# Four leading modulation panels: DVE chain or TensorE column groups, with v and q multiplied in halves around them

## What is computed

```python
c_act = jax.nn.silu(c)
for l in range(DEPTH):
    mod = (c_act @ ada_w[l] + ada_b[l]).reshape(bsz, 6, 1, D_MODEL)
    sh1, sc1, g1, sh2, sc2, g2 = (mod[:, i] for i in range(6))
    h = rms_norm(x, norm1_g[l]) * (1.0 + sc1) + sh1
    # l == 0: even_mixer
    proj = h @ w_in
    u, v, q, k, vd = split_cols(proj, (SGU_WIDTH, SGU_WIDTH, DIFF_QK, DIFF_QK, DIFF_V))
    ...
    x = x + g1 * y
    h = rms_norm(x, norm2_g[l]) * (1.0 + sc2) + sh2
    x = x + g2 * grouped_moe(h, router_w, router_b, moe_w_gu[l], moe_w_down[l])
return rms_norm(x, final_g)
```

## Time and profile before

| | us |
|---|---|
| median of 3 runs | 1056.99 |
| lowest and highest of the 3 | 1055.16, 1057.19 |
| the profiled execution, whole | 1058.29 |
| its span, first to last instruction | 1056.2 |
| mean granted TensorE clock | 0.931 |
| PE busy, of the span | 951.6 |
| DVE busy | 416.0 |
| ACT busy | 171.0 |

### The profile page before, as it was taken

One profiled execution on the slowest core, in us unless ns is written; L12 is line 12 of the kernel. 1 busy time (PEld: TensorE's weight loads), 2 busy tenths in 40 slices (PEclk: granted clock), 3 DMA queues, 4 the chain that ended last, 5 costly groups with the idle time before them and its releaser, 6 DMA issues.

```text
span 1056.2 us, 13230 instructions
## 1 busy us (share of the span) xinstructions
PE 951.6 (90%) x5496; PEld 609.1 (58%) x5496; DVE 416.0 (39%) x984; ACT 171.0 (16%) x416; POOL 13.0 (1%) x51
## 2 busy tenths in 40 slices
PE   2799789899999899896999989898789999999994
PEld 2476544565555465453868777765466556555551
DVE  4856575442141311312796645534351111111112
ACT  2121120221111011101101312332201111111101
POOL 1000000000000000000000000000000000000000
PEclk8699899799999899898999988988879999999998
DMA  9996644667999999999377312280209899999931
GB/s 353 387 372 246 238 161 157 239 235 294 406 408 409 404 409 407 407 397 365 138 262 286 108 62 102 81 318 1 79 24 404 328 409 409 409 408 409 408 158 42
DMA packets 96081, 294.16 MB, mean 278 GB/s; under 512 B 2448, under 2 KB 3088, under 8 KB 96016
## 3 DMA queue, kind: packets, MB, share of 16 engines
q1 hardware_dynamic: 95184, 289.89, 71.4%
q10 hardware_dynamic: 688, 2.82, 0.7%
q0 software_dynamic: 144, 0.52, 0.1%
HBM read 292.18 MB, written 1.05 MB: 278 GB/s over the span
## 4 chain that ended last, share of the span: by engine, by line
PE 49%; issue 26%; DVE 11%; DMA 6%; SPq 6%; ACT 3%; POOL 0%; DVEq 0%; POOLq 0%
PE bank L630 13%; PE bank L626 9%; PE bank L815 8%; SPq L406 5%; DVE gb L1210 4%; DMA ring<-w_gu_dram 4%; PE bank L830 3%; PE bank L806 2%; PE bank L844 2%; PE bank L659 2%; PE bank L681 2%; PE bank L566 2%; PE bank L574 1%; DMA ring<-ada_w_dram 1%; PE bank L788 1%
## 5 line engine op out<-in xcount | busy, mean ns | idle before, releaser
L815 PE MATMUL bank<-ring,scr 128*64 128x256 f32 x2176 | 253.2, 387 | 9.5 <-DMA ring<-w_gu_dram 9.5
L815 PEld LDWEIGHTS bank<-ring,scr 128*64 128x64 f32 x2176 | 154.8, 139 | 102.1 <-issue 20.6
L630 PE MATMUL bank<-hT,ring 128*128 128x256 f32 x640 | 149.7, 396 | 0.0
L630 PEld LDWEIGHTS bank<-hT,ring 128*128 128x128 f32 x640 | 127.1, 200 | 19.1 <-issue 0.5
L830 PE MATMUL bank<-ring,scr 128*64 128x512 f32 x544 | 122.6, 592 | 0.0
L1210 DVE SCALAR_TENSOR_TENSOR gb<-ring,small,gb 128x512 f32<-128x512 f32 x140 | 105.5, 754 | 5.0
L1660 DVE TENSOR_TENSOR scr<-bank,scr 128x256 f32<-128x256 f32 x34 | 14.4, 424 | 202.7 <-ACT scr L1150 202.7
L806 PEld LDWEIGHTS bank<-scr,xh 128*128 128x128 f32 x576 | 68.5, 195 | 24.5 <-issue 22.0
L806 PE MATMUL bank<-scr,xh 128*128 128x128 f32 x576 | 74.8, 285 | 2.3 <-DVE scr L1632 2.3
L830 PEld LDWEIGHTS bank<-ring,scr 128*64 128x64 f32 x544 | 38.9, 137 | 64.4 <-issue 59.8
L1132 ACT ACTIVATE scr<-bank 128x256 f32<-128x256 f32 (+1 forms) x52 | 23.4, 450 | 300.1 <-PE bank L823 237.3
(11 more groups left out here) (217 smaller groups left out, 685.5 us busy)
## 6 DMA issues: line engine op xcount, KB each, us to landing
ring<-w_gu_dram SPq DMA_DIRECT2D x64, 2048.0 KB, 21.7
ring<-w_down_dram SPq DMA_DIRECT2D x32, 2048.0 KB, 21.1
ring<-ada_w_dram SPq DMA_DIRECT2D x24, 2048.0 KB, 18.1
ring<-od_w_in_dram SPq DMA_DIRECT2D x9, 2048.0 KB, 13.6
ring<-ev_w_in_dram SPq DMA_DIRECT2D x5, 2048.0 KB, 17.4
ring<-ev_w_out_dram SPq DMA_DIRECT2D x2, 2048.0 KB, 9.7
ring<-od_w_out_dram SPq DMA_DIRECT2D x2, 2048.0 KB, 11.0
xs<-x_dram ACTq DMA_DIRECT2D x1, 1024.0 KB, 6.1
```

What stands on the lines that cost most here:

```text
L630: ins = pe.matmul(banks[h][:, m * 256:(m + 1) * 256], w[:, c, (2 * h + m) * P:(2 * h + m + 1) * P], x_part[:, c, :], start=(c == 0 and m = ...
L815: ins = pe.matmul(b[64 * m:64 * m + 64, 256 * u:256 * u + 256], h[:, c, :], w[:, c, 512 * u + 256 * m:512 * u + 256 * m + 256], start=(fir ...
```

## The change

- **PE takes the four leading panels.** `ada_row(n)` multiplies a panel directly: eight matmuls, one for each chunk c, whose weights are the column `cact[:, c]` repeated 32 times and whose output is the 32 partitions `32 * (c % 4)` of bank 6. So the chunks go in turn to four column groups of the array, twice each. DVE copies the bank to SBUF (L1785), and `ada_row_sum` sums over the partitions as before, with a column of 1/32, as each sum stands there 32 times. DVE's 32 instructions of 128x512 for these panels are gone; 4 copies come in.
- **Order of the panels.** They load as ada 0, 2, v, q, 1, 3. After ada 0 and 2, DVE makes `hT` for the chunks 0 to 3, PE multiplies the first halves of v and q, then rows 1 and 3, then the second halves with ACT's `hT`.
- **Small transfers.** `sgw` follows ada 1; `rows` (0.7 MB) leaves ACT's queue for SP's, behind ada 3.
- **Banks.** In layer 0 v goes to banks 4 and 5, the others to banks 0 to 3 in turn, so that the transposed x in banks 2 and 3 can wait for ACT.
- `keep_busy(2)` of this stage is gone.

```diff
-PRE = [[("ada", 0), ("ada", 1), ("ada", 2), ("ada", 3), ("in", "v"), ("in", "q"), ("ada", 4), ("ada", 5), ("in", "k"),
+FIRST_ADA = [0, 2, 1, 3]
+PRE = [[("ada", 0), ("ada", 2), ("in", "v"), ("in", "q"), ("ada", 1), ("ada", 3), ("ada", 4), ("ada", 5), ("in", "k"),
...
+            return bank[f % 4] if l else bank[4 + f] if f < 2 else bank[(f - 2) % 4]
...
+            def ada_row(n):
+                pl = pre_place(0, ("ada", FIRST_ADA[n]))
+                if n:
+                    pe.wait_ge(acc_ready, n)
+                pe.wait_ge(panel_in[pl.slot], pl.landed)
+                for c in range(KC):
+                    g = 32 * (c % 4)
+                    ins = pe.matmul(bank[6][g:g + 32, :], cact[:, c:c + 1].to_broadcast([P, 32]), panel(pl.slot)[:, c, :],
+                                    start=(c < 4), stop=(c >= 4), skip_group_check=True)
+                ins.then_inc(panel_done[pl.slot], 1)
+
+            def ada_row_sum(n):
+                take(misc)
+                pe.wait_ge(acc_ready, n + 1)
+                for m in range(4):
+                    ins = pe.matmul(bank[7][:, m:m + 1], acc_even[n % 2][:, m * P:(m + 1) * P], thirty_second,
+                                    start=True, stop=True)
+                give(misc, ins)
...
-                for f in range(6):
+                fill(0, 0)
+                fill(0, 2)
+                for n in (2, 3):
+                    ada_row(n)
+                    ada_row_sum(n)
+                pe.wait_ge(sguw_masked, 1)
+                transposes([sgw[:, g, :] for g in range(4)])
+                for f in (1, 3, 4, 5):
                     fill(0, f)
...
-            ada(0)
-            for j in range(1, 4):
-                ada(j)
-                ada_out(0, j - 1)
-            ada_out(0, 3)
-            open_phase(0)
-            norm(0)
+            for n in range(4):
+                pl = pre_place(0, ("ada", FIRST_ADA[n]))
+                dve.wait_ge(panel_done[pl.slot], pl.done)
+                dve.tensor_copy(acc_even[n % 2], bank[6][:, :]).then_inc(acc_ready, 1)
+                ada_out(0, FIRST_ADA[n])
+                if n == 1:
+                    scale_up(0, 0, range(4)).then_inc(half_ready, 1)
+                    dve.wait_ge(half_ready, 1)
+                    hT_rows(0)
+            scale_up(0, 0, range(4, 8)).then_inc(x_ready, 1)
```

More of the change, by code:

```diff
@@ L276, in trunk @@
         minus_half = sm(892, 1)
+        thirty_second = sm(893, 1)
         qT = [view(0, 4, 256), view(1024, 4, 256)]
@@ L328, in trunk @@
         cact_ready = sem("cact_ready")
+        part_ready, acc_ready, half_ready = (sem(n) for n in ("part_ready", "acc_ready", "half_ready"))
         ada_step = sem("ada_step")
@@ L393, in wait_fill, with fill_bank @@
             eng.wait_ge(panel_done[pl.slot], pl.done)
-        def fill_bank(f):
-            return bank[f % 4]
+        def fill_bank(f, l=1):
+            return bank[f % 4] if l else bank[4 + f] if f < 2 else bank[(f - 2) % 4]
         block = ctx.enter_context(nc.Block())
@@ L418, in load_pre @@
                     load(pl, panel(pl.slot), src, PRE_AT[l] + k >= PANELS)
-                    if l == 0 and k == 3:
+                    if l == 0 and k == 4:
                         sp.dma_start(sgw, sgu_w[0].rearrange("g t s -> t g s")).then_inc(sguw_in, 16)
+                    if l == 0 and k == 5:
+                        sp.dma_start(row, rows.partition_broadcast(P)).then_inc(rows_in, 16)
                         sp.dma_start(rb_row[:, :], router_b.partition_broadcast(P)).then_inc(rb_in, 16)
@@ L619, in fill @@
                 for c in range(4 * half, 4 * half + 4):
-                    if p == 0 and c == 0:
-                        pe.wait_ge(hT_dve, 8 * l + 4)
+                    if p == 0 and l == 0 and c < 4:
+                        pe.wait_ge(hT_dve, c + 1)
+                    if p == 0 and l == 1 and c == 0:
+                        pe.wait_ge(hT_dve, 12)
                     if p == 0 and c >= 4:
@@ L964, in _ @@
             pe.wait_ge(consts, 2)
[L965 to L973, removed]
+            norm_T(0)
+            pe.wait_ge(cact_ready, 1)
+            pe.wait_ge(part_ready, 1)
+            for n in (0, 1):
+                ada_row(n)
+                ada_row_sum(n)
             even()
@@ L1053, in even @@
                     wait_fill(act, 0, h)
-                    act.activation(vg[:, h, :], fill_bank(h)[:, :], ACT.Gelu_apprx_tanh).then_inc(fill_act[0], 1)
+                    act.activation(vg[:, h, :], fill_bank(h, 0)[:, :], ACT.Gelu_apprx_tanh).then_inc(fill_act[0], 1)
                 for h in range(2):
@@ L1060, in even @@
                             r = slice(64 * k, 64 * k + 64)
-                            ins = act.activation(qz[k][r, c, :], fill_bank(2 + h)[r, m * 256:(m + 1) * 256], ACT.Copy,
+                            ins = act.activation(qz[k][r, c, :], fill_bank(2 + h, 0)[r, m * 256:(m + 1) * 256], ACT.Copy,
                                                  scale=0.125 * 4.0 ** (c + 1))
@@ L1068, in even @@
                     wait_fill(act, 0, 8 + h)
-                    act.activation(uu[:, h, :], fill_bank(8 + h)[:, :], ACT.Gelu_apprx_tanh).then_inc(fill_act[0], 1)
+                    act.activation(uu[:, h, :], fill_bank(8 + h, 0)[:, :], ACT.Gelu_apprx_tanh).then_inc(fill_act[0], 1)
                 for k in range(4):
@@ L1164, in _ @@
             act.dma_start(xs[:, :, :], x.rearrange("(t p) d -> p t d", p=P)).then_inc(x_in, 16)
-            act.dma_start(row, rows.partition_broadcast(P)).then_inc(rows_in, 16)
             act.wait_ge(cols_in, 16)
@@ L1258, in rstd_of, with hT_rows @@
                 dve.tensor_scalar(rms_t, ssq, 1.0 / D, RMS_EPS, ALU.mult, ALU.add).then_inc(pow_asked, 1)
+            def hT_rows(ph):
+                l, s = ph // 2, ph % 2
+                for c in range(4):
+                    dve.wait_ge(xT_ready, 4 * ph + c // 2 + 1)
+                    dve.tensor_scalar(hT[:, c, :], bank[c // 2][:, 256 * (c % 2):256 * (c % 2) + 256],
+                                      scale(l, s, c), shift(l, s, c),
+                                      ALU.mult, ALU.add).then_inc(hT_dve, 1)
             def norm(ph):
@@ L1266, in norm @@
                 dve.wait_ge(x_ready, ph + 1)
[L1267 to L1271, removed]
+                hT_rows(ph)
             def scores(l, n, j, s_, nm, d):
```

20 lines of the change are left out of this document (11 added, 9 removed).

## The result

| | before | changed |
|---|---|---|
| median, us | 1056.26 (8 runs, 1051.03 to 1059.33) | 1048.49 (8 runs, 1041.59 to 1049.43) |
| profiled execution, us | 1058.29 | 1048.95 |
| its span, us | 1056.2 | 1047.0 |
| mean granted clock | 0.931 | 0.942 |
| DVE busy, us | 416.0 | 396.1 |

The ratio is 0.992, with a 95% interval of 0.9893 to 0.9947. Timed again after the other experiments (e12), the changed kernel gave 0.9905 (0.9869 to 0.9941). The prediction said 1047.0.

The account below looks back on a forecast made before the run. Bound: DVE's panel sums before v, then a chain moving together. 16.5 us less before v, 8.2 more between halves, about 2 from clock: gain 10.1, taken as 10.0; 1058.29 to 1048.3 profiled, 1047.0 median; range 1043 to 1054.

Parts of the forecast that it names:

- The bound: Up to v, DVE's panel sums bound the kernel; behind k all moves together, so what k gains, the whole gains.
- The rows: Each ada_row of 16 records on PE, four groups side by side: 1.75 us at full clock, 3.5 at half.
- The rival by the weight loads: In PE's rows, weight loads make the groups overlap imperfectly: 2.2 us a row, gain 7.7, 1049.3 us; chance 0.12.
- the 2.3 us that the prediction estimates beside it: Cost of a PE row by the Trainium skill's 3.07 for four row groups: 2.3 us, gain 7.3.
- The first row: Row 0 on PE, behind the transposes, runs at half clock: 3.5 us, from 16.1 to 19.6.
- the first rival: Clock is up from row 0 on: row 0 saves 1.75 us, gain 11.8, 1045.2 us; chance 0.16.
- Full clock from there: After row 0, from 19.6 us, PE runs at full clock: v's halves 7.0 us each, k ends at 76.1.
- the second rival: Clock stays down until inside v, as copies and sums break the dense work: gain 4.5, 1052.5 us; chance 0.18.
- The copies and sums: After each row, DVE's bank copy 0.8 us and PE's sum 1.05; last sum to PE's next start 1.0.
- Transfers and queues: Panel landings hidden by 3.2 us at least; SP's hold on vd costs nothing; DVE ready 3 us before k.
- The whole: Gain of 10.0 us at k arrives at the end: profiled execution 1048.3 us, median 1047.0; chance 0.37.
- The chances: Outcome for the whole kernel: faster (below 1054.9 us) 0.87, within 0.07, slower 0.06.

Follow-up runs that it names:

- e12: The changed kernel run again, unaltered, after the other experiments; 1043.97 us, 0.9905 of the kernel before.
- e5: Changed kernel's panel order kept, but DVE sums the four leading panels again instead of rows on PE; 1048.81 us, 0.9935 of the kernel before.
- e4: Changed kernel with its four rows on PE, but panels in the old order and v, q whole; 1047.15 us, 0.9896 of the kernel before.
- e2: Changed kernel with the leading panels on two column groups of 64 instead of four of 32; 1054.68 us, 0.9984 of the kernel before.
- e3: Changed kernel with the leading panels on all 128 columns, no groups; 1065.63 us, 1.0091 of the kernel before.
- e10: Changed kernel with useless matmuls filling PE's waits in the head, the gating stage and under the copies of rows 1, 3; 1039.75 us, 0.9859 of before.
- e1: Changed kernel with two keep_busy(1) added, under the second row's copy and behind its sum; 1044.55 us, 0.9889 of the kernel before.

## Why the prediction was right, and where it was not

- **The bound.** DVE's chains ahead of v, and a chain behind k that moves as a whole: right. e5 and e4 show it from both sides, e2 and e3 by the price.
- **The rows.** 1.75 us forecast, 1.92 measured; the term is 0.17 low in three rows, 0.5 us in all. The step from pairs to fours does cost a little (3.7 of 4). The rival by the weight loads, 2.2 us, is out, and so is the 2.3 us that the prediction estimates beside it.
- **The first row.** Forecast 3.5 at half clock, with the rise behind it; measured 2.81, and 1.92 to 2.99 in the other traces with four groups: the rise in pace comes inside it, or ahead of it in e10, where the transposes already took 3.34 instead of 3.65. That lies between the forecast and the first rival, and I had both.
- **Full clock from there.** This is the step that failed in the profiled execution: the clock fell at 24.3 us and again at 51.7, 4.8 us in sum (9.99 + 8.83 - 14.0). k ended at 80.4, near what the second rival gives there (81.7), though its cause was another: not a clock that stayed down but one that rose and fell again. In the second trace of the same kernel k ended at 76.5, near the forecast's 76.1, but not by the forecast's steps: the first row took 2.03 instead of 3.5, and the second half of v 8.56 instead of 7.0, as the clock fell there too. The forecast should have had both as one case with a spread.
- **The copies and sums.** 0.90 from a row's end to its sum, and 1.02 to 1.05 for a sum: as forecast (0.8 and 1.05). From the last sum to v 1.1 us, forecast 1.0.
- **Transfers and queues.** No row of PE in the changed kernel's head waits for a panel; e4 put the landings of the fourth panel and of v at 28.5 and 34.5, where the cadence has 28.4 and 34.4. SP's long hold on vd cost nothing. DVE waited 4.73 us for k (forecast 3, with k earlier).
- **The whole.** 10 us forecast for the profiled execution, 9.3 found, of which 5.8 at k. Medians: 7.8 in the first series, and by the second ratio 10. The forecast for the profiled execution, 1048.3 against 1048.95, was close by luck: k ended 4.3 us later than forecast, and the clock gave back 3.3 us between 512 and 620 us (107.6 against 110.9) that it had taken ahead. The range needed the 2 us either way that it had for this, and single executions would have needed 4.
- **The chances.** The prediction's 0.87 for "faster" is a slip: 0.83 with half of 0.08 and half of 0.05 is 0.895.

## What to carry to other kernels

When a chain on one engine holds the first product back, ask what is the earliest moment at which that product's own operand is there. Here either of two means moved k's end from 86.2 to about 79 us, and both together gave no measurable time more. Take the simpler one. And where an edit strips an engine's wait down to short copies and one-column sums, price the stretch at both clocks. Dense work under the waits costs nothing if the wait is long enough, but time the unaltered kernel again before crediting the filling with a gain: e12 took back e1's.

## What the runs showed of the hardware

- Four column groups of 32 with four different moving operands of 512 float32 columns ran at 3.7 times the serial rate (1.92 against 7.03 us for 16 records), two groups at 1.93 (3.65).
- A granted clock of 1.00 at the start of a trace is not to be taken for pace: in e5 the stretch 20 to 27 us reads 1.00, but sums there took 1.84 and 1.85 us, as at half clock, and the first half of v 9.48.
- The same code gets the clock's falls in different places from one execution to the next (first half of v 9.99 and 7.11 us in two traces of the changed kernel). With the change the slower executions have the lower mean clock (e4: 1039.88 us at 0.949, 1051.45 at 0.940). In the kernel before the mean clock doesn't tell (1050.41 us at 0.937, 1060.45 at 0.939 in one series), so what makes its spread stays open.
